# A fused projection by seven half-sized products in place of eight, with its token operands read back from DRAM

## The reference, cut to what matters

```python
D_MODEL = 1024; SEQ = 2048; DEC_BATCH = 8; DEC_SEQ = 8
h = rms_norm(x, g_norm)                 # float32, 2048 + 64 rows of 1024
z = jnp.einsum('btd,dn->btn', h, w_in)  # all columns of w_in
(qa, ka, va, fa, ga, qb, kb, vb, lrb, gb, xc, bc, cc, gc, mg) = split_columns(z)
# three mixers read z: forgetting attention, gated linear attention (GLA), short convolution
# yb = ... * silu(gb);  u = cc * xc;  yc = bc * conv(u) * silu(gc);  gates = sigmoid(mg)
```

## Time and profile before

| | |
|---|---|
| time, median of 3 | 3746.3 us (3746.05 to 3747.52) |
| profiled execution: its span | 3747.3 us (the page gives no other time of its own) |
| PE busy | 3585.3 us, 96% |
| DVE, ACT, POOL busy | 50%, 48%, 38% |
| projection | first product matmul at 16.0 us, last at 1783.7 us |
| DMA | 157 GB/s over the span |

### The profile page before, as it was taken

One profiled execution on the slowest core, in us unless ns is written; L12 is line 12 of the kernel. 1 busy time (PEld: TensorE's weight loads), 2 busy tenths in 40 slices (PEclk: granted clock), 3 DMA queues, 4 the chain that ended last, 5 costly groups with the idle time before them and its releaser, 6 DMA issues. The chain is left out here.

```text
span 3747.3 us, 54477 instructions
## 1 busy us (share of the span) xinstructions
PE 3585.3 (96%) x17931; PEld 2823.4 (75%) x17931; DVE 1867.7 (50%) x3105; ACT 1810.5 (48%) x3712; POOL 1423.5 (38%) x1072
## 2 busy tenths in 40 slices
PE   8999999999999999999799999899999999799999
PEld 7788888788878888888566666677777777588787
DVE  3134423332123543322557665588888888544432
ACT  4224423445323443543566767677777777311222
POOL 0011122220011122310477777577777777322200
PEclk9999999999999999999799999999999999899999
DMA  4234334324233334333201211699999999544422
GB/s 164 77 120 132 115 128 145 122 96 139 97 108 115 127 132 155 118 126 88 61 18 40 60 38 63 225 329 335 340 335 334 319 338 326 208 155 162 150 90 76
DMA packets 378555, 590.40 MB, mean 158 GB/s; under 512 B 93381, under 2 KB 114485, under 8 KB 378298
## 3 DMA queue, kind: packets, MB, share of 16 engines
q1 hardware_dynamic: 366146, 579.94, 45.9%
q10 hardware_dynamic: 11584, 5.13, 0.5%
q0 software_dynamic: 576, 2.10, 0.2%
HBM read 475.25 MB, written 111.83 MB: 157 GB/s over the span
## 5 line engine op out<-in xcount | busy, mean ns | idle before, releaser
L996 PE MATMUL prj_z_ps<-prj_w_hi,prj_h_hi 128*128 128x512 f32 x2312 | 923.9, 400 | 2.8 <-DVE prj_w_lo L792 2.7
L998 PE MATMUL prj_z_ps<-prj_w_hi,prj_h_lo 128*128 128x512 f32 x2312 | 902.6, 390 | 0.0
L997 PE MATMUL prj_z_ps<-prj_w_lo,prj_h_hi 128*128 128x512 f32 x2312 | 901.2, 390 | 0.0
L1912 POOL TENSOR_TENSOR sa_v_lo<-sa_v_raw,sa_v_hi 128x1024 fp32r<-128x1024 f32 x256 | 609.1, 2402 | 219.7 <-DVE sa_v_hi L2051 219.2
L998 PEld LDWEIGHTS prj_z_ps<-prj_w_hi,prj_h_lo 128*128 128x128 f32 x2312 | 434.3, 188 | 93.7
L996 PEld LDWEIGHTS prj_z_ps<-prj_w_hi,prj_h_hi 128*128 128x128 f32 x2312 | 435.2, 188 | 90.0 <-DVE prj_w_lo L792 5.7
L997 PEld LDWEIGHTS prj_z_ps<-prj_w_lo,prj_h_hi 128*128 128x128 f32 x2312 | 435.3, 188 | 84.8
L1408 POOL TENSOR_TENSOR pa_p_lo<-pa_probs,pa_p_hi 128x512 fp32r<-128x512 f32 (+1 forms) x320 | 367.6, 1164 | 160.9 <-ACT pa_p_hi L1421 143.5
L2045 DVE TENSOR_TENSOR sa_kT_lo<-sa_t_ps,sa_kT_hi 128x512 fp32r<-128x512 f32 x512 | 345.5, 686 | 141.9 <-ACT sa_kT_hi L1934 138.7
L424 POOL TENSOR_TENSOR prj_dist<-prj_cum 128x256 f32<-128x256 f32 x132 | 88.6, 671 | 793.5 <-DVE prj_cum L863 793.5
L1934 ACT CAST sa_kT_hi<-sa_t_ps 128x512 fp32r<-128x512 f32 x512 | 291.1, 590 | 128.6 <-PE sa_t_ps L2198 120.0
(11 more groups left out here) (330 smaller groups left out, 6417.7 us busy)
## 6 DMA issues: line engine op xcount, KB each, us to landing
arena_k_raw<-in_cache_k_dram SPq DMA_DIRECT2D x512, 256.0 KB, 4.1
sa_v_raw<-in_cache_v_dram SPq DMA_DIRECT2D x512, 256.0 KB, 4.3
arena_w_raw<-in_w_main_dram SPq DMA_DIRECT2D x272, 256.0 KB, 4.2
z_scratch<-prj_z_sb SPq DMA_DIRECT2D x272, 256.0 KB
arena_mg<-z_scratch SPq DMA_DIRECT2D x51, 512.0 KB, 4.4
arena_cu<-extp_scratch SPq DMA_DIRECT2D x48, 256.0 KB
arena_x_in<-in_x_all_dram SPq DMA_DIRECT2D x17, 512.0 KB, 3.7
prj_aux<-z_scratch SPq DMA_DIRECT2D x34, 256.0 KB, 2.8
```

The costliest lines, as they stand in the source:

```text
L996: pe.matmul(out, h_hi[:, slot_of(t), k], hi, start=(k == 0), stop=False)
L997: pe.matmul(out, h_hi[:, slot_of(t), k], lo, start=False, stop=False)
L998: mm = pe.matmul(out, h_lo[:, slot_of(t), k], hi, start=False, stop=(k == KC - 1))
L1912: pool.tensor_tensor(v_lo[:, w % 2, at], v_raw[:, w % RING, at], v_hi[:, w % 2, at].bitcast(F32), ALU.subtract).then_inc(vlo_ready, 1)
```

## The change

One block, Z_VA, is still computed in full (units "va": 24 matmuls each, 17 of them). The 16 others go in 8 pairs, `PAIRED`. For a pair, the prompt's z is a 2x2 arrangement of blocks: token halves (tiles 0 to 7, 8 to 15) by the two column blocks; h is token halves by contraction halves (HK = 4 slices each). One level of Strassen's method in Winograd's form gives the four quarters from 7 products (`PHASES`) in place of 8, each 8 token tiles x 4 slices x 3 matmuls. A phase f of pair j has 8 units of 12 matmuls; phases 1, 4, 5 and 6 put out finished tiles. The sample tile takes units of its own, "sa", after phases 0 and 4: 16 matmuls each, with high and low part side by side as one stationary operand. In all 481 units.

- The seven token operands (sums and differences of quarters of h) are made once, in the va part: POOL forms the sums (`token_sum`), PE turns them, ACT and DVE split them, SP stores them to `h_ops` in DRAM (56 operands of 512 KB). From then on SP loads one operand per unit of 12 matmuls into a ring of 4 (`h_ring`), 448 loads.
- The weight sums T1 to T4 are formed by POOL in place in the raw tiles (`weight_sum`, 16 subtractions a pair). Each weight slice is loaded once. The split weights' ring shrinks from 9 to 7 slices, and 28 slices a pair are split where 2 x 16 were.
- Products are combined as they leave PSUM: ACT copies phase 0 to `xy`; DVE adds phases 1 to 6 from PSUM (phase 5 twice). Sigmoids and silu products then work from SBUF to SBUF.
- The tail is computed per tile in the va part, by 8 matmuls of 256 columns with 64 stationary columns.
- GLA chunks start every 20 units, steps 1.5 units apart; convolutions every 12 units. `load_next` is issued at the first unit of phase 3 of the last pair, with 33 units left to compute.

```diff
-    GROUPS = [range(0, 9), range(9, TILES)]
-    W_RING, RAW, Z_RING, PS_RING = 9, arena.W_RAW, 4, 3
+    HT = PROMPT_TILES // 2
+    HK = KC // 2
+    PAIRED = [(Z_QKB, Z_VB), (Z_XC, Z_BC), (Z_CC, Z_GC), (Z_GA, Z_GB), (Z_QA, Z_KA)] + \
+        [(Z_MG + 2 * i, Z_MG + 2 * i + 1) for i in range((N_BLOCKS - Z_MG) // 2)]
+    PHASES = 7
+    W_RING, Z_RING, PS_RING, H_RING, STAGES = 7, 5, 3, 4, 3
+    UNITS = [("va", i) for i in range(TILES)]
+    for j in range(len(PAIRED)):
+        for f in range(PHASES):
+            UNITS += [("mm", j, f, tp) for tp in range(HT)]
+            if f in (0, 4):
+                UNITS.append(("sa", j, f))
...
+    START = UNIT_OF["mm", 1, 0, 0] + 4
+    PERIOD = 20
...
-    NEXT_LOADS = len(UNITS) - 4
+    NEXT_LOADS = UNIT_OF["mm", len(PAIRED) - 1, 3, 0]
...
+            def weight_sum(name, j, k):
+                if name == "t1":
+                    pool.tensor_tensor(w_raw[:, k], raw2[:, 0, k], w_raw[:, k], ALU.subtract).then_inc(t1_ready, 1)
...
+            def load_operand(q):
...
+                    sp.wait_ge(z_done, UNIT_OF[("mm",) + STREAMED[q - STREAM - H_RING]] + 1)
...
+                sp.dma_start(dst, h_ops[f, tp]).then_inc(h_loaded[slot], 16)
...
+                if f == 2:
+                    dve.tensor_tensor(x, src, x, ALU.add).then_inc(dve_evicted, 1)
+                elif f == 3:
+                    dve.tensor_tensor(v, src, x, ALU.add).then_inc(dve_evicted, 1)
+                elif f == 5:
+                    dve.tensor_tensor(out_of(u), src, v, ALU.add)
+                    dve.tensor_tensor(x, src, x, ALU.add).then_inc(dve_evicted, 1)
+                else:
+                    dve.tensor_tensor(out_of(u), src, v if f == 4 else x, ALU.add).then_inc(dve_evicted, 1)
...
             def unit(u):
...
+                pe.wait_ge(h_loaded[q % H_RING], 16 * ((q - STREAM) // H_RING + 1))
+                for k in range(HK):
+                    s = slice_of(j, f, k)
...
+                    pe.matmul(out, h[:, 0, k], hi, start=(k == 0), stop=False)
+                    pe.matmul(out, h[:, 0, k], lo, start=False, stop=False)
+                    mm = pe.matmul(out, h[:, 1, k], hi, start=False, stop=(k == HK - 1))
```

More of the change, by code:

```diff
@@ L191, in project @@
     HALO = CONV_W - 1
     LAST = TILES - 1
+    ORDER = list(range(HT)) + [LAST] + list(range(HT, PROMPT_TILES))
     w_view = w_main.rearrange("(k p) (b n) -> b k p n", p=P, n=BLK)
[L194 to L197, removed]
-    UNIT_OF = {x: u for u, x in enumerate(UNITS)}
+    UNITS = [("va", i) for i in range(TILES)]
@@ L199, in project @@
+    O_OF = {u: n for n, u in enumerate(sorted(OUTS))}
+    UNIT_MAKING = {bt: u for u, bt in OUTS.items()}
     GATES = range(Z_MG, N_BLOCKS)
-    ON_VECTOR = (Z_CC, Z_GA, Z_GB, Z_GC)
+    SILUS = (Z_GA, Z_GB, Z_GC)
     AUX = {Z_CC: Z_XC, Z_GC: Z_BC}
[L203 to L207, removed]
-        return 2 if b in (Z_KA, Z_VA) or (b == Z_CC and t == PROMPT_TILES - 1) else 1
-    STORED = [16 * sum(stores(x) for x in UNITS[u % Z_RING:u + 1:Z_RING]) for u in range(len(UNITS))]
@@ L211, in project @@
[L211 to L221, removed]
@@ new lines, in project, with on_scalar, stores @@
+    PROD, PROD_OF = listed(PRODUCTS)
+    AUXED, AUX_OF = listed(AUX)
+    def on_scalar(u):
+        x = UNITS[u]
+        return (x[0] == "va" and ORDER[x[1]] != LAST) or (x[0] == "mm" and x[2] == 0)
+    EVICTED = [sum(on_scalar(v) == on_scalar(u) for v in range(u + 1)) for u in range(len(UNITS))]
+    SAMPLED = [sum(u in OUTS and OUTS[u][1] == LAST for u in range(v + 1)) for v in range(len(UNITS))]
+    def stores(u):
+        b, t = OUTS[u]
+        return 2 if b in (Z_KA, Z_VA) or (b == Z_CC and t == PROMPT_TILES - 1) else 1
@@ new lines, in project, with slice_of @@
+    STORED = {}
+    for u, n in O_OF.items():
+        STORED[u] = 16 * stores(u) + (STORED[sorted(OUTS)[n - Z_RING]] if n >= Z_RING else 0)
+    OUT_UNITS = sorted(OUTS)
+    def slice_of(j, f, k):
+        return (j * PHASES + f) * HK + k
+    SLICES = len(PAIRED) * PHASES * HK
+    W_FIRST = 3 * HK + 1
+    FREED = {}
+    for j in range(len(PAIRED)):
+        for f in range(PHASES):
+            for k in range(HK):
+                if f in (0, 4) or k < HK - 1:
+                    FREED[slice_of(j, f, k)] = len(FREED) + 1
@@ new lines, in project @@
+    PART = {"r11": (0, 0), "r12": (1, 0), "r21": (0, 1), "r22": (1, 1)}
+    OPS = []
+    for i in range(TILES):
+        if i < HT:
+            OPS.append([("ring", 0, i), ("ring", 1, i)])
+        elif i == HT:
+            OPS.append([("sample", n, None) for n in range(3)])
+        else:
+            tp = i - HT - 1
+            OPS.append([("ring", 3, tp), ("ring", 6, tp), ("stage", 5, tp), ("stage", 2, tp), ("stage", 4, tp)])
+    TURN = [[sum(map(len, OPS[:i])) + n for n in range(len(OPS[i]))] for i in range(TILES)]
@@ L224, in project @@
+    PERIOD = 20
+    BASE = [START + PERIOD * c for c in range(TILES)]
+    CHUNK_STEP = {}
+    for c, at in enumerate(BASE):
+        for step in range(-3, 14 if c < LAST else 14 + DEC_BATCH):
+            CHUNK_STEP.setdefault(at + 3 * step // 2, []).append((c, step))
+    CONV_AT = {UNIT_OF["mm", 3, 0, 0] + 12 * i: i for i in range(TILES)}
     CONV_STEPS = 2 * CONV_W - 1
@@ new lines, in tail_unit @@
+            def tail_unit(i):
+                n = 2 * tail_cols(i)
+                out = tail_ps[i % 2][0:64, 0:n].rearrange("p (a t) -> p a t", a=2)
+                if i == 0:
+                    pe.wait_ge(wlo_ready, W_FIRST - HK)
+                wait_from(pe, tail_ready, i - 1)
+                for part in range(2):
+                    w = 0 if part == 0 else 1 if i <= HT else 2
+                    for k in range(HK):
+                        if i == HT:
+                            h = hs[:, part, k]
+                        else:
+                            h = h_ring[:, ring_at(i, part) % H_RING, :, k]
+                        mm = pe.matmul(out, tail_w[:, w * HK + k].rearrange("p a n -> p (a n)"), h,
+                                       start=(part == 0 and k == 0), stop=(part == 1 and k == HK - 1))
+                mm.then_inc(tail_done, 1)
```

957 lines of the change are left out of this document (667 added, 290 removed).

## The result

| | before | after |
|---|---|---|
| time, median | 3746.9 us (4 runs, 3746.05 to 3747.78) | 3691.7 us (4 runs, 3689.39 to 3693.9) |
| ratio, 95% interval | | 0.9848 [0.9835, 0.9861] |
| profiled span | 3747.3 us | 3691.7 us |
| first and last product matmul | 16.0 and 1783.7 us | 26.0 and 1726.1 us |
| behind the last one | 1963.6 us | 1965.6 us |

A forecast was written before the change was run, and what follows sets the result against it. PE issuing matmuls was taken to bound the projection. 3747.3 us less 200 saved, plus 77 of waits (12 + 25 + 16 + 8 + 12 + 4), gave 3624, stated as 3623 us; range 3558 to 3705.

The forecast's parts named there:

- the third rival: DVE and POOL hold each other up all through the pairs: 3710 us, chance 0.15; sign: line 1144 or 1263 well above 0.85.
- The saving of 200 us: PE in the projection: 904 fewer matmuls (-204.9 us), tail -5, turns +10, together -200, giving 3547 us without added waits.
- The va part: Tiles 8 to 15: transfers of 9.3 or 11.0 us a tile against PE's 8.5; +12 us, bounds 0 and 30.
- hand-over: From the va part to the pairs: an added drain, given as the reason for the va part's upper bound of 30 us.
- DVE in the silu pairs: Phases 4 and 5 of (CC, GC) and (GA, GB): DVE overloaded and slowed by POOL; +25 us, bounds 0 and 60.
- Phase edges: Where phases meet: PE waits for the last slice's split, 1 us for each of 16 sample units; +16, bounds 0 and 45.
- POOL in phase 1: Lumped weight sums ahead of a GLA level, 2 us in each of four pairs with convolution; +8, bounds 0 and 30.
- DMA: Pairs: operand loads plus stores, with 16 key units storing twice, exceed the unit's time; +12 us, bounds 0 and 35.
- side estimate of +5: Pairs' transfers at the skill page's 358 GB/s: a unit takes 3.0 us and only the key units stick out, +5.
- load_next: Its six loads stand in front of operand loads: PE can go on 11 us, next operand after 15; +4, bounds 0 and 13.
- All fits: First rival, whole projection: queues smooth the waits, only the va part and key units remain; 3556 us, chance 0.25.
- The stream as bound: Second rival, in the pairs: PE waits for h_loaded at a unit's first matmul; at 225 GB/s 3822 us, chance 0.08.

The follow-up runs named there:

- e1: The changed kernel with the load of a unit's second factor issued one unit earlier: ratio 0.9779 to the kernel before, 26 us under the changed kernel.
- e3: The changed kernel with va-part statistics and normalisation put behind the next tile's last high and low parts: ratio 0.9829, 7 us under the changed kernel.
- e4: The changed kernel with the pad rows' zeros sent in six pieces and load_next's six loads issued one at a time: ratio 0.9802, 17 us under it.
- e7: e5 with ScalarE and DVE doing the slice's split before the GLA step and product: ratio 0.9648, 15 us under e5, 3616.6 us.
- e8: e5 with the second tile's turns moved behind the first unit's matmuls: ratio 0.9683, 1.5 us under e5, no difference.
- e9: e7 with POOL's convolution cut to 8 of its 512 columns, the rest left out: ratio 0.9592, 21 us under e7.
- e2: The changed kernel with POOL doing its GLA step before its weight sums in each unit: ratio 0.9819, 11 us under the changed kernel.
- e10: e7 with each streamed operand loaded by half, its low parts left out: ratio 0.9623, 9 us under e7 (13 by the medians).
- e5: The changed kernel with the four edits of e1, e2, e3 and e4 together: ratio 0.9687, 60 us under the changed kernel.

## Why the prediction was right or wrong

The sum had 77 us of waits; some 145 came. The time still lies in the stated range, but by luck: the range reached that far for the third rival, whose sign is absent. The edits for causes outside the sum (e1, e3, e4) give back 50 of the 68 us, 4 of which the sum had.

**The saving of 200 us: right.** Its steps (5376 matmuls, 2.72 us a unit, later stages unchanged) are in the rows above. No run reaches the 3547 us of a kernel without waits; e7, with all its work, comes to 3617.

**The start: left out.** I compared stretches from 16.0 us; the first product matmul came at 26.0. e8 shows that the 10 us are no separate cost: what is won at the start is given back in the first units. They belong to the va part.

**The va part: step right, size wrong.** +12 forecast, 34 measured, 44 with the start. I priced engines and bytes and took a value between them. e3 shows 11 us of order: ACT stood at an x tile's statistics with casts for PE behind them. My upper bound of 30 was named a "hand-over", not that.

**DVE in the silu pairs: the failed step.** +25 forecast from DVE's throughput and POOL, some 70 measured (42 and 27 over the price, with the phase edges of these pairs in them). Of these 27 are e1's: the diff moved `load_aux` from two units ahead to one behind, and shortened the unit from 5.44 to 2.72. The forecast counted DVE's products and never asked when the load for them is issued: a wait that it put at nothing without a reason. The transfer isn't in its list of bytes either. The part that I did count holds: POOL's convolution costs pair 3 12 us (e9), and one product of 0.69 us took 1.67 beside it:

```profile
912.18 1.74 POOL L568 TENSOR_TENSOR arena_cu<-arena_cu,arena_taps 128x512 f32<-128x512 f32 x1
...
912.80 1.67 DVE L1191 TENSOR_TENSOR prj_z_sb<-prj_z_sb,prj_sig 128x512 f32<-128x512 f32 x1
```

The Trainium skill's page "SBUF — State Buffer", section "Who interferes with whom", states that a DVE instruction with two SBUF inputs contends with a GpSimd instruction that reads SBUF. This row (1.67 us) and e9 (0.94 against 0.63 us) agree.

**Phase edges: right in size and cause.** +16 forecast, 15 by e7, and the cause as told: what stands ahead of the last split in both queues. The place is another: the forecast had 1 us for each of 16 sample units, but pairs 2 and 3 gain 8 and 7 us of it.

**POOL in phase 1: right in size.** +8 forecast, 11 by e2, 8 of them in phase 1 of pairs 2, 3 and 4. It reaches PE at GLA's matmuls; why ACT's waits hardly fell isn't settled.

**DMA: right in size, as far as shown.** +12 forecast, 9 to 13 by e10, which took away half of the operands' bytes and nothing else. The prediction's side estimate of +5 is mis-added: a key unit of 1.33 MB at 358 GB/s takes 3.7 us, 0.56 over 3.15, and 16 of them make 9. DMA acts less on the operands than on other late transfers.

**load_next: mis-sized, pads overlooked.** +4 forecast, 9.5 measured; and `store_pads`, in the new kernel a single burst among the operand loads, cost 7 more (8.3 in its phase, of which 1.5 came back behind it) that I had not seen. I gave PE four units of cover for 12.6 us of loads, but the loads and stores already queued count too.

**The clock: no term.** 22 us in after. It seems no cause of its own: it follows the waits and goes with them (112, 72, 67, 26 slow matmuls in after, e5, e7, e9).

**The rivals.** All fits: no. The stream as bound: no, 232 to 296 GB/s in the pairs; operands are waited for at two bursts. The time lies in the third rival's stretch (3665 to 3738), yet its sign isn't there: line 1144 has a mean of 0.84 us, line 1263 of 0.52, under the 0.85 that I set:

```profile
L1263 DVE TENSOR_TENSOR prj_qE<-prj_q_bd,prj_dec 64x128 f32<-64x128 f32 x230 | 119.3, 519 | 93.8 <-ACT prj_dec L1046 92.2
L1144 DVE TENSOR_TENSOR prj_w_lo<-prj_raw,prj_w_hi 128x512 fp32r<-128x512 f32 x128 | 105.1, 821 | 96.0 <-ACT prj_w_hi L966 95.0
```

DVE and POOL hold each other up in places, not all through.

## What to carry to other kernels

When a change halves the length of a work unit, recompute in microseconds every lead that the code counts in units: a load issued "one unit ahead" may no longer cover its landing, and in an in-order queue it delays everything behind it. A wait's row names the last link only: PE's largest group here named a GLA copy, while for a third of it (37.3 us, 24.6 in e1) the cause was a DMA further back in DVE's queue. And a sum of engine times and bytes finds the floor well; the waits above it lay in order, in bursts and in the clock behind each wait, which edits of a line or two take back.
